# Row norm's root moved behind the first MLP matmul, and a new order of work in two attentions

## Time and profile before

| | us |
|---|---|
| median of 3 runs (lowest, highest) | 1856.22 (1854.83, 1856.53) |
| the profiled execution, its own time | 1861.01 |
| its span, first to last instruction | 1859.1 |
| TensorE matmul busy | 1810.3 |
| ScalarE / VectorE / GpSimd busy | 848.2 / 832.6 / 834.8 |
| mean granted TensorE clock, of full speed | 0.992 |

### The profile page before, as it was taken

One profiled execution on the slowest core, in us unless ns is written; L12 is line 12 of the kernel. 1 busy time (PEld: TensorE's weight loads), 2 busy tenths in 40 slices (PEclk: granted clock), 3 DMA queues, 4 the chain that ended last, 5 costly groups with the idle time before them and its releaser, 6 DMA issues.

```text
span 1859.1 us, 26998 instructions
## 1 busy us (share of the span) xinstructions
PE 1810.3 (97%) x9064; PEld 1505.4 (81%) x9064; DVE 832.6 (45%) x1384; ACT 848.2 (46%) x1795; POOL 834.8 (45%) x598
## 2 busy tenths in 40 slices
PE   8999999999999999999999999999999999999998
PEld 7788888887888888888888888877888888887776
DVE  4688888888304443235430033050253311534644
ACT  4655555554325655324442244253533332456652
POOL 4654555577353132435444444445454444442322
PEclk9999999999999999999999999999999999999999
DMA  5732121222133121423233333324232223221211
GB/s 175 138 90 69 56 68 56 60 64 57 57 102 120 52 79 51 132 89 102 83 98 102 91 102 91 102 81 159 81 108 80 85 86 102 80 71 57 63 40 57
DMA packets 46223, 159.85 MB, mean 86 GB/s; under 512 B 4763, under 2 KB 7195, under 8 KB 45884
## 3 DMA queue, kind: packets, MB, share of 16 engines
q1 hardware_dynamic: 38592, 140.53, 24.7%
q10 hardware_dynamic: 7548, 18.20, 4.0%
HBM read 152.42 MB, written 6.29 MB: 85 GB/s over the span
## 4 chain that ended last, share of the span: by engine, by line
PE 81%; DVE 8%; issue 4%; ACT 4%; POOL 1%; DMA 1%; DVEq 0%; ACTq 0%; POOLq 0%
PE main L300 60%; PE main L328 4%; PE aux L802 4%; PE aux L656 2%; PE main L1800 2%; PE aux L789 2%; DVE u_acc L2002 1%; PE aux L772 1%; PE aux L372 1%; DVE x_res L564 1%; PE aux L773 1%; DVE y_all L2080 1%; PE aux L1888 1%; PE aux L647 1%; ACT w_hi L259 1%
## 5 line engine op out<-in xcount | busy, mean ns | idle before, releaser
L263 POOL TENSOR_TENSOR w_lo<-raw,w_hi 128x512 fp32r<-128x512 f32 x504 | 700.7, 1397 | 895.0 <-ACT w_hi L259 883.1
L259 ACT ACTIVATE w_hi<-raw 128x512 fp32r<-128x512 f32 x486 | 304.5, 630 | 696.7 <-PE main L300 683.7
L300 PE MATMUL main<-w_hi,a_hi 128*128 128x512 f32 x736 | 304.2, 413 | 2.3 <-ACT vv L1547 1.5
L300 PE MATMUL main<-w_hi,a_lo 128*128 128x512 f32 x736 | 288.1, 391 | 0.0
L300 PE MATMUL main<-w_lo,a_hi 128*128 128x512 f32 x736 | 287.3, 390 | 0.0
L300 PE MATMUL main<-a_hi,w_hi 128*128 128x512 f32 x576 | 231.2, 401 | 1.6 <-ACT u_raw L1296 1.6
L300 PE MATMUL main<-a_hi,w_lo 128*128 128x512 f32 x576 | 225.2, 391 | 0.0
L300 PE MATMUL main<-a_lo,w_hi 128*128 128x512 f32 x576 | 224.9, 390 | 0.0
L300 PEld LDWEIGHTS main<-w_hi,a_lo 128*128 128x128 f32 x736 | 138.1, 188 | 30.3
L300 PEld LDWEIGHTS main<-w_hi,a_hi 128*128 128x128 f32 x736 | 138.5, 188 | 28.4 <-ACT vv L1547 1.9
L300 PEld LDWEIGHTS main<-w_lo,a_hi 128*128 128x128 f32 x736 | 138.8, 189 | 23.0
(11 more groups left out here) (320 smaller groups left out, 3111.7 us busy)
## 6 DMA issues: line engine op xcount, KB each, us to landing
raw<-w_stream_in SPq DMA_DIRECT2D x264, 512.0 KB, 3.6
x_res<-x_in ACTq DMA_DIRECT2D x8, 512.0 KB, 5.1
rel_rows<-rel_row ACTq DMA_DIRECT2D x1, 4096.0 KB, 44.3
bias<-rel_rows ACTq DMA_DIRECT2D x2, 1536.0 KB, 8.3
out<-x_res SPq DMA_DIRECT2D x4, 512.0 KB, 2.7
bgate<-b_gate_in ACTq DMA_DIRECT2D x4, 256.0 KB, 5.8
ln_g<-ln_g_in ACTq DMA_DIRECT2D x1, 1024.0 KB, 4.7
ln_b<-ln_b_in ACTq DMA_DIRECT2D x1, 1024.0 KB, 6.8
```

The costliest lines, as they stand in the source:

```text
L259: eng.activation(w_hi[:, k, :], raw[:, k, :], ACT.Copy).then_inc(hi_done, 1)
L263: eng.tensor_tensor(w_lo[:, k, :], raw[:, k, :], w_hi[:, k, :].bitcast(F32), ALU.subtract).then_inc(lo_done, 1)
L300: mm = eng.matmul(mb[m][:, :], lhs, rhs, start=(first and k == 0 and n == 0), stop=(last and k == KT - 1 and n == 2))
```

## The change

It has four parts. (1) First boundary: `op1` transposes `x_res` instead of a scaled copy; the norm's squares come later, the four roots are turned into a row by four matmuls behind half step 14 of the first MLP panel, copied by ScalarE to `root_row`, and VectorE does `max(v, 0) * root_row` on each bank of all eight `w_mlp_in` panels in place of ScalarE's relu. (2) First attention: the last head moves into step 0 of the next panel, and the loop over j is written out. (3) Both attentions: other orders on ScalarE and VectorE; `before(m)` runs ahead of the `bank_free` wait. (4) Entry of the second attention: `act_take_kv` one `make_hi` earlier, and the transposes of the values go behind step 1 of the query panel.

```diff
@@ main_step
             for m in range(4):
+                if before is not None:
+                    before(m)
                 if first and k == 0 and free_wait:
                     eng.wait_ge(bank_free, (og - 1) * 4 + m + 1)
-                if before is not None:
-                    before(m)
@@ act_heads(self, eng, j, p, gate)
                 for t in range(8):
-                    if t:
-                        self.act_turned(eng, j, t - 1, [0, 1])
-                    self.act_exp(eng, j, t, [0, 1])
-                    if t:
-                        self.act_turned(eng, j, t - 1, [2])
-                    self.act_exp(eng, j, t, [2, 3])
-                    if t:
-                        self.act_turned(eng, j, t - 1, [3])
+                    if t == 0:
+                        self.act_exp(eng, j, 0, [0, 1])
+                    else:
+                        for c in range(NT):
+                            self.act_turned(eng, j, t - 1, [c])
+                            if t == 1 and c < 2:
+                                self.act_exp(eng, j, 0, [c + 2])
+                            if t > 1:
+                                self.act_exp(eng, j, t, [c])
+                            elif c >= 2:
+                                self.act_exp(eng, j, 1, [2 * c - 4, 2 * c - 3])
                     make_hi(eng, p, t)
-                self.act_turned(eng, j, 7)
+                for c in range(NT):
+                    self.act_turned(eng, j, 7, [c])
+                    gate(c)
@@ dve_query (second attention)
+                if op is not None:
+                    op.dve(eng, [0, 1])
+                self.dve_take_q(eng, j, [1])
                 self.dve_logits(eng, j, 0, [0, 1])
                 if op is not None:
                     op.dve(eng, [2])
-                self.dve_take_q(eng, j, [1])
...
@@ dve_heads(self, eng, ch, j, take)
                     if t < 7:
                         self.dve_logits(eng, j, t + 1)
+                    else:
+                        for m in range(3):
+                            take(m)
                     if t:
                         self.dve_out(eng, j, t - 1)
+                take(3)
+                self.dve_den(eng, ch, j, 7)
@@ objects of the first boundary
-        norm1 = RowNorm(1, fb, junk, 12, 1)
-        op1 = HalfOperand("op1", fb, [to_a(lambda k: col("pre_mlp", k))])
+        norm1 = RowNorm(1, None, junk, 12)
+        op1 = HalfOperand("op1", x_res, [to_a(lambda k: col("pre_mlp", k))])
+        def act_turn_bank(act, res, norm, op, p, spare, og):
+            for k in range(NSP):
+                spare_hi(act, spare, p, k)
+            res.act_sq_bank(act, 0, og, p - 1)
+            for k in range(NSP, KT):
+                spare_hi(act, spare, p, k)
+            res.act_sq_bank(act, 1, og, p - 1)
+            res.act_sq_bank(act, 2, og, p - 1)
+            for i in range(4):
+                op.act(act, i)
+            res.act_sq(act, 1, og, [3])
+            for i in range(4, 2 * KT):
+                op.act(act, i)
+                if i in (4, 6, 8, 10):
+                    norm.act_one(act, (i - 4) // 2, lambda e, m: res.wait_new(e, m))
+                if i >= KT and i < KT + NSP:
+                    next_hi(act, p + 1, i - KT)
+            act.wait_ge(root_turned, 1)
+            act.activation(root_row[:, :], ab[0][:, :], ACT.Copy, scale=1.0).then_inc(root_set, 1)
+        def dve_turn_bank(dve, ch, res, norm, op, og, p):
+            for m in range(3):
+                res.dve_ms_one(dve, m)
+                res.dve_gain_bank(dve, m)
+                res.dve_wait_gain(dve, m)
+                res.dve_add_one(dve, m)
+            for i in range(2):
+                op.dve(dve, i)
+            res.dve_take(dve, 1, og=og, p=p, ms=[3])
+            op.dve(dve, 2)
+            res.dve_ms_one(dve, 3)
+            res.dve_gain(dve, ch, 1, [3])
+            res.dve_add_one(dve, 3)
+            for i in range(3, 2 * KT):
+                op.dve(dve, i)
+                if i == 11:
+                    norm.dve_mean(dve)
@@ gpsimd
-            pool_turn(pool, res1, norm1, P_MLP, spare1)
+            pool_turn_late(pool, res1, norm1, P_MLP, spare1)
@@ scalar, MLP
-                        act.activation(relu[:, m, :], mb[m][:, :], ACT.Relu).then_inc(bank_free, 1)
@@ scalar, entry of the second attention
-            hi(P_KV2 + 1, [6, 7])
-            act.wait_ge(step_done, 8 * P_KV2 + 8)
+            hi(P_KV2 + 1, [6])
+            att2.act_take_kv(act, P_KV2, O_KV2)
+            hi(P_KV2 + 1, [7])
             load(dist[:, :], d["dist"], dist_landed)
-            att2.act_take_kv(act, P_KV2, O_KV2)
@@ head_panel
+                    if i == 14 and root_of is not None:
+                        pe.wait_ge(norm_rs, root_of.i * NT + NT)
+                        for m in range(NT):
+                            row = pe.matmul(ab[0][:, m * P:(m + 1) * P], root_of.root(m).broadcast_to((P, P)), ident, start=True, stop=True)
+                        row.then_inc(root_turned, 1)
@@ tensor: first attention, second attention
+            query_panel(P_QG + 2, O_QG + 2, ao, lambda m: first_logits(att1, 1, m, O_QG + 2), last_head=last_of(att1, 0))
...
+                    main_step(pe, P_GA, k, *ao(k), False, O_GA, before=before_ga, after=after_ga)
...
-            att2.pe_turn_v(pe, O_KV2)
-            query_panel(P_QZ, O_QZ, ao, lambda m: first_logits(att2, 0, m, O_QZ))
+            query_panel(P_QZ, O_QZ, ao, lambda m: first_logits(att2, 0, m, O_QZ), second=lambda: att2.pe_turn_v(pe, O_KV2))
...
             def under_q1(m):
-                if m < 2:
-                    op_o2.pe(pe, [m + 2])
+                if m == 0:
+                    pe.wait_ge(z_gate, one_up(NT))
+                    op_o2.pe(pe, [0, 1])
+                elif m < 3:
+                    op_o2.pe(pe, [m + 1])
@@ vector, MLP
+                        dve.scalar_tensor_tensor(relu[:, m, :], mb[m][:, :], 0.0, root_row[:, :], ALU.max, ALU.mult).then_inc(bank_free, 1)
@@ vector, second attention (the first one alike)
-                att2.dve_heads(dve, ch, j)
-                for m in range(NT):
+                def take_z(m):
                     wait_full(dve, j * 2 + (P_QZ + 1), j * 2 + (O_QZ + 1), m)
                     dve.tensor_copy(zt[:, m, :], mb[m][:, :]).then_inc(bank_free, 1)
-                att2.dve_den(dve, ch, j, 7)
-                att2.dve_out(dve, j, 7)
+                att2.dve_heads(dve, ch, j, take_z)
                 for m in range(NT):
+                    if m == 3:
+                        att2.dve_out(dve, j, 7)
                     dve.wait_ge(z_tanh, j * 4 + m + 1)
                     ch(dve.scalar_tensor_tensor(gt[:, m, :], gt[:, m, :], 1.0, zt[:, m, :], ALU.add, ALU.mult))
+                for m in range(NT):
                     o = o2[:, m, j * NCOL:(j + 1) * NCOL]
                     dve.tensor_tensor(o, o, gt[:, m, :], ALU.mult).then_inc(z_gate, 1)
```

More of the change, by code:

```diff
@@ L911, in dve_query, with dve_heads @@
                     op.dve(eng, [2])
[L912 removed]
+                self.dve_take_q(eng, j, [2])
+                self.dve_logits(eng, j, 0, [2, 3])
                 if op is not None:
                     op.dve(eng, [3])
[L915 to L916 removed]
                 self.dve_take_q(eng, j, [3])
[L919 removed]
+            def dve_heads(self, eng, ch, j, take):
                 for t in range(8):
@@ L1473, in _, with g_gate @@
                 make_hi(act, j * 2 + (P_QG + 1), 7)
-                att1.act_heads(act, j, j * 2 + (P_QG + 2))
-                for m in range(4):
+                def g_gate(m):
                     act.wait_ge(bank_free, j * 8 + (4 * (O_QG + 1) + m + 1))
                     act.activation(gt[:, m, :], gt[:, m, :], ACT.Tanh, scale=0.5).then_inc(g_tanh, 1)
+                att1.act_heads(act, j, j * 2 + (P_QG + 2), g_gate)
             for n in range(2):
@@ L1514, in _ @@
                 with act.Fori(0, 4) as i:
-                    for m in range(4):
-                        wait_full(act, i + base, i + ob, m)
-                        act.wait_ge(f_ready, one_up(i * 4 + 16 * h))
-                        act.activation(relu[:, m, :], mb[m][:, :], ACT.Relu).then_inc(bank_free, 1)
                     make_hi(act, i + (base + 1), 7)
@@ L1607, in _ @@
                     make_hi(act, j * 2 + (P_QZ + 1), k)
-                if j:
-                    op_o2.act(act, [0, 1])
                 for m in range(3):
                     att2.act_take_q(act, j, j * 2 + P_QZ, j * 2 + O_QZ, [m])
-                    if j and m < 2:
-                        op_o2.act(act, [m + 2])
+                    if j:
+                        op_o2.act(act, [[0, 1], [2], [3]][m])
                 for k in range(4, 7):
@@ L1617, in _, with z_gate_tanh @@
                 make_hi(act, j * 2 + (P_QZ + 1), 7)
-                att2.act_heads(act, j, j * 2 + (P_QZ + 2))
-                for m in range(4):
+                def z_gate_tanh(m):
```

(37 more changed lines are left out.)

33 lines of the change are left out of this document (14 added, 19 removed).

## The result

The kernel after takes **1842.48 us** in the median of 4 runs (1842.23 to 1844.90), the kernel before 1856.38 in 4 runs (1854.83 to 1859.51). The ratio is 0.9926, 95% interval 0.9909 to 0.9943: **13.9 us faster**, where 15.6 were forecast. The profiled executions differ by more: spans of 1859.1 and 1840.4, 18.7 us. Both differences need an account.

What follows compares the result with a forecast made beforehand. TensorE, busy 1810 us, was taken to bound the kernel, so only its waits and slower clock counted. Gains of 4.2 + 3.9 + 1.3 + 2.7 + 1.4 + 1.4 + 0.7 = 15.6 us took 1856.2 to 1840.6 us, range 1837 to 1848.

Steps and rivals of the forecast that it cites:

- The first boundary: Start of the first MLP panel: 6.1 us lost time removed, less 0.7, 1.1 and 0.1 of new costs: 4.2 us gained.
- gap at half step 3: First boundary: half step 3 still waits for the fourth tile, behind take, squares, gain, root and add on VectorE: 0.7 us.
- the relu's wait: End of the first MLP panel: VectorE's first relu follows the row's copy, so next panel's bank 0 waits 0.1 us.
- The relu at nothing: MLP panel ends: 32 relus moved to VectorE at 0.68 us cost nothing, hidden up to 0.96 us an instruction.
- Rival C: Eight MLP panel ends: VectorE's relu takes 1.79 us beside GpSimd, costing 27.2 us in all: 1867.8 us; chance 0.03.
- The entry: Start of the second attention: query panel's step 0 follows at once, wait and lower clock go: 3.9 us gained.
- The attentions: Both attentions, new orders: 0.7 us in the first; 1.3, 2.7, 1.4 and 1.4 at places in the second: 7.5 gained.
- the two `issue` waits: Second attention, next panel's step 0, twice: three takes now come ahead of head 6's output: 2.7 us gained for both.
- o_lo: Second attention at 1741.53, where VectorE is late with it: transposes come later, z's products sooner: 1.4 us gained.
- Rival A: Both attentions: the waits come back one step later, 5 of 7.5 us lost: 1845.6 us; chance 0.13.
- The last head under a step: First attention, both j: last head moved into the next panel's step 0 is no cheaper: 0.0 us, ends -0.5 and 1.0.
- Rival B: First boundary: the clock falls in spite of the shorter gap, 3 us less gained: 1843.6 us; chance 0.11.

Runs made afterwards that it cites:

- the forced stop: Kernel after, with the norm's first two squares on ScalarE put between the transposes and its first operand, so TensorE stands some 2 us: 1846.26 us, ratio 0.9938.
- experiment 5: Kernel after, with two more waits on GpSimd in the first and second boundary, holding two subtractions until residual tiles are done: 1840.83 us, ratio 0.9914.
- experiment 9: Kernel after with GpSimd's two subtractions held at the first and second boundary, plus the root's four matmuls behind half step 12, not 14: 1840.35 us, ratio 0.9905.
- experiment 8: Kernel after, with the gate panel's four takes behind the output of head 6 again, in both attentions: 1848.63 us, ratio 0.9951.
- experiment 7: Kernel after, with the last head of the first attention alone behind step 7 as before, for both j: 1843.27 us, ratio 0.9927.
- experiment 3: Kernel before with only the new entry of the second attention: ratio 0.9986, 2.6 us gained.
- experiment 1: Kernel before, unchanged, run and profiled once more: 1857.05 us, ratio 0.9998.

## Why the prediction was right, and where it was off

**The first boundary** is 4.1 in the profile for 4.2, and 3.7 alone in the runs. Its steps: third tile's gap gone, yes; clock at 1.00, in all nine profiled executions of the new boundary without the forced stop, against one of four of the old one; gap at half step 3, 0.47 idle and 0.7 by the starts of the matmuls, for 0.7, but the reason given (four steps in a row in VectorE's queue) is wrong, since experiment 5 removes it by moving GpSimd alone. The same holds for the gap of 1.41 in the earlier trace rows, which was put down to VectorE's take and add of the bank: the same queue has no gap when its add takes 1.29. The root's matmuls cost 0.9 for 1.1, no wait at them. The one step too low is the relu's wait, 0.5 for 0.1: the row's copy ends at 896.44 and the first relu starts at 896.79, 0.5 later than where the row is early (experiment 9).

**The relu at nothing** is right: at 0.69 no wait but the first, at 1.32 a bank 15.5 us lost. The bound of 0.96 lies between the two, but nothing was run near it. Rival C is out by its own row, 679 to 692 ns in all 32.

**The entry** won 3.9 in the profile and 2.6 in the runs. **The attentions** won 7.4 alone for 7.5 forecast in parts 2 and 3; by the timelines the first values, the gated outputs and the two `issue` waits are within 0.3 of their terms, o_lo gave 1.8 for 1.4. Of the 0.7 in the first attention 0.5 came from the first heads. Only the takes were taken apart (experiment 8); that the other orders act by the way the prediction tells rests on the waits that went. Rival A (waits that come back one step later) isn't seen: no wait over 0.4 is left inside the attentions. The last head under a step was put at 0.0, and against the kernel before it saves 0.1 and 0.0; left alone among the new orders it would cost 0.3 (experiment 7).

**What failed** is the sentence that carried the sum to the median: "the median of the runs lies 4.8 lower, and the gain is the same there". The execution that was profiled was the slowest one of before then shown. Sixty more executions of this kernel were timed beside the experiments, each with its mean granted clock: their median is 1857.9 us, 45 of them have a clock of 0.995 or 0.996, and the five with the profiled one's 0.992 took 1860.9 to 1861.6. So it stands for the slow end of them. Its lost time held two things that other executions have less of: the lower clock behind each stop (1.9 us less at the first boundary in experiment 3, 1.6 less at the entry in experiment 1) and the long add at the second boundary (1.5 with the step behind it). The first belongs to terms of the sum (6.1 and 4.2), so the gain at these two places is between 2.2 and 4.1, and between 2.3 and 3.9, by execution. Alone in the runs, the two parts with a clock in their terms fell short by 0.5 and 1.3, the attentions, which have none, by 0.1. That is about the 1.7 us between 15.6 and 13.9, but each of these has an interval of 1.7 or more to either side, so it fits the account and doesn't prove it. A mean clock doesn't say at which stop the clock fell, so how often each place has it, and how often the long add occurs, stays open in the runs that weren't profiled. Rival B's clock isn't seen in any execution without the forced stop. Its reading of the kernel before was off: at the first boundary TensorE had stood 1.90 us, not over 2, and a third place with a fallen clock was left out, the third boundary with its wait of 2.26.

## What to carry to other kernels

A profile is one execution: profile the same kernel twice before a stretch at the lower clock, or an instruction at twice its length, goes into a sum at full value. When an instruction has two lengths in one profile, look at what the other engine started just before it, and hold that one back if it has time; two semaphore waits won 1.5 us here by the timeline, about as much as one of the reorderings in the second attention. A factor that commutes with what follows can be moved behind the matmul, and what decides its cost there is the pace at which banks fill, not the engine's busy share. Times taken in different groups of runs are compared by their ratios to one kernel that stands in both groups: here the plain medians made 6.2 us of 4.6.

## What was not expected of the hardware

- At the first and second boundary VectorE's add of 128x1024 takes 1.28 us alone and 2.22 to 2.35 when GpSimd's subtraction began 0.02 to 0.15 earlier; when VectorE is first, the subtraction takes 1.80 to 2.01 for 1.29. A lead of 0.02 us decides.
- VectorE's scaling of 128x1024, which has one SBUF tensor as input, took 0.74 to 0.76, and 1.12 to 1.14 beside GpSimd: it is held as well.
- The same stops of 1.9 and 1.1 us left the clock at 0.72 in three executions and at 1.00 in one. The stop of 2.27 at the old entry was followed by a lower clock in two of four executions, the stop of 2.3 at the third boundary in 11 of 14.
